# A hybrid decoder layer on one NeuronCore: the first MLP product by Strassen's rule, its outputs spilled to DRAM, the second product in four chunks

## The chip, the core and the metric

The kernel runs on one core of a Trainium2 chip. The metric is the device time of one execution in microseconds (us). Engines are named as in the profile: PE (TensorE; PEld is its weight load), DVE (VectorE), ACT (ScalarE), POOL (GpSimd), SP (SyncE, which here only issues DMAs).

## The reference, cut to what matters

```python
h2 = rmsnorm(x, g_pre_mlp)                     # x: 1024 prompt tokens and 8 decode tokens, 1024 features
f = jnp.square(jax.nn.relu(h2 @ w_ff1)) @ w_ff2    # w_ff1 1024 x 4096, w_ff2 4096 x 1024
x = x + rmsnorm(f, g_post_mlp)

def rmsnorm(x, g):
    return x * lax.rsqrt(jnp.mean(x * x, axis=-1, keepdims=True) + EPS) * g
```

Before this stand the projections, a pooled branch, an mLSTM, a memory attention, the gated merge and the out-projection `merged @ w_out`, whose normalised result is added to x. All is float32.

## The kernel before, in words

All activations lie transposed: features on the 128 partitions (KD = 8 tiles), the N = 1032 tokens along the free axis, cut into NG = 3 groups of G = 344 (`tok[g]`). A float32 product is made of three fp32r passes: each operand is split into a high part (a copy into fp32r) and a low part (the operand minus its high part), and `product` (L573 to L582) issues hi*hi, lo*hi and hi*lo for each 128-deep block into one PSUM bank. So a block of 128 features by 344 tokens over 1024 inputs takes 8 x 3 = 24 matmuls, each with its own weight load.

Weights come as one stream of slabs of 128 x 1024 (512 KB) on SP's queue into two slots of `w_raw`; POOL splits each slab (`split`, L466 to L480: `w_hi` by a multiplication with ones, then `w_lo`), a few by ACT and POOL. SP loads the next slab once the one before it is split.

The MLP runs after the out-projection (units UNIT_OUT on). There ACT takes z out of PSUM and squares it, DVE sums the squares, one matmul with ones per group sums over partitions, ACT takes the root, DVE inverts it and scales (`z_inverse`, `z_scale`), and POOL adds the result to x (L540). Then, for the second norm, ACT squares x tile by tile, PE sums the squares by 24 matmuls with ones (L840), ACT takes the root, DVE inverts it (L1532) and multiplies x by gain and reciprocal (STT, L1181), ACT makes `h_hi`, DVE and POOL make `h_lo` (L1538, L546). The groups follow each other: the first MLP matmul of group 0 waits for group 0's low parts alone.

The first product makes 32 blocks of 128 features, the second 8 blocks; both go in turns, 512 hidden features at a time. `ff1` on PE (L842) issues 4 blocks x 3 groups of 24 matmuls; ACT takes the ReLU (L906), DVE squares (L1547), ACT copies the high part (L1142), DVE makes the low part (L1549), all in SBUF. `ff2` (L848) then multiplies the 512 hidden features: 8 blocks x 3 groups of 12 matmuls, each added by DVE to `acc` (L1559). That is 2304 matmuls for either product, 4608 in all, each 344 columns wide. Every engine works through its own program in order, and semaphores tie them; a group's bank is reused when `s_group_free[g]` says that its reader is done.

At the end `f_last` orders the last groups by token group; ACT squares `acc`, PE sums the squares by 8 matmuls per group (`f_mean`), ACT takes the root, DVE inverts, scales, and DVE and POOL add x1, and SP stores o_y.

## Time and profile before

| | us |
|---|---|
| median of 3 runs | 2166.03 (2163.33 to 2166.05) |
| profiled execution, device time | 2168.67 |
| its span, first to last instruction | 2166.9 |
| PE busy | 2045.7 (94%) |
| DVE, POOL, ACT busy | 957.6, 801.8, 459.7 |
| mean granted TensorE clock | 0.966 |

The span of the profiled execution is 2166.9 us, and 1.8 us lie around it. Busy time counts an engine's instructions; a matmul's record overlaps the next one's, so PE's pace is read from start times or from a stretch's count, not from a single duration. The granted clock is in tenths of full speed: 1.00 is 2.4 GHz and half of it 1.2 GHz.

### The profile page before, as it was taken

The page shows a single profiled execution, that of the slowest core. Times are in us where ns is not written, and L with a number is a line of the kernel's source. Part 1 is how long each engine was busy: PE and PEld are TensorE (multiplying, and loading weights), DVE is VectorE, ACT ScalarE, POOL GpSimd, SP SyncE. Part 2 cuts the span into 40 slices and gives each one's busy share as a digit, 9 for nine tenths or more (in the row PEclk, how much of TensorE's full clock was granted, in tenths as well). Part 3 has the DMA queues.
Part 4 walks back from the last instruction along what each step waited for, and adds up shares of the span by engine and source line. Part 5 has one row for each costly group of instructions (what it writes and reads, how often), then busy time and mean ns, then how long its engine had stood idle before and what let it go on. Part 6 is the DMA issues. An engine that isn't in the chain of part 4 may idle for free.

```text
span 2166.9 us, 32354 instructions
## 1 busy us (share of the span) xinstructions
PE 2045.7 (94%) x12613; PEld 1989.7 (92%) x12613; DVE 957.6 (44%) x1864; ACT 459.7 (21%) x880; POOL 801.8 (37%) x405
## 2 busy tenths in 40 slices
PE   5799999999999999999899989599999999999996
PEld 3799999999999999999789889399999999999995
DVE  6602552045303550255756742964334343343426
ACT  4411220122012211122056422431102011010101
POOL 4553323322333333332512323753434343333433
PEclk8899999999999999999789999799999999999998
DMA  3221331123211331133544331211111111111132
GB/s 137 69 79 44 132 140 50 40 104 134 79 49 60 133 124 40 40 136 127 211 140 140 104 127 39 98 40 49 49 39 50 49 49 40 49 49 49 40 117 79
DMA packets 64140, 180.13 MB, mean 83 GB/s; under 512 B 6648, under 2 KB 22264, under 8 KB 63400
## 3 DMA queue, kind: packets, MB, share of 16 engines
q1 hardware_dynamic: 57664, 154.46, 20.8%
q10 hardware_dynamic: 6376, 24.14, 2.8%
q8 instruction: 86, 1.41, 0.3%
q14 instruction: 14, 0.11, 0.0%
HBM read 141.83 MB, written 36.75 MB: 82 GB/s over the span
## 4 chain that ended last, share of the span: by engine, by line
PE 85%; DVE 9%; issue 2%; ACT 2%; DMA 1%; POOL 1%; SPq 0%; DVEq 0%; ACTq 0%; POOLq 0%
PE bank L580 78%; DVE acc L1181 2%; PE bank L708 1%; PE bank L711 1%; DVE x_in L1181 1%; PE bank L700 1%; PE bank L663 1%; PE bank L706 1%; PE bank L747 1%; DMA x_in<-xT 1%; PE bank L780 0%; PE bank L840 0%; PE bank L687 0%; PE bank L803 0%; PE bank L716 0%
## 5 line engine op out<-in xcount | busy, mean ns | idle before, releaser
L580 PE MATMUL bank<-h_hi,w_hi 128*128 128x344 f32 x2520 | 824.4, 327 | 26.9 <-DVE h_lo L1196 14.2
L580 PE MATMUL bank<-h_lo,w_hi 128*128 128x344 f32 x2520 | 809.5, 321 | 0.0
L580 PE MATMUL bank<-h_hi,w_lo 128*128 128x344 f32 x2520 | 806.8, 320 | 0.0
L477 POOL TENSOR_TENSOR w_hi<-w_raw,ones 128x1024 fp32r<-128x1024 f32 x152 | 288.7, 1900 | 1165.9 <-PE bank L580 1153.2
L580 PEld LDWEIGHTS bank<-h_hi,w_hi 128*128 128x128 f32 x2520 | 477.4, 189 | 33.8 <-issue 16.1
L580 PEld LDWEIGHTS bank<-h_hi,w_lo 128*128 128x128 f32 x2520 | 476.9, 189 | 1.2
L580 PEld LDWEIGHTS bank<-h_lo,w_hi 128*128 128x128 f32 x2520 | 476.9, 189 | 0.0
L479 POOL TENSOR_TENSOR w_lo<-w_raw,w_hi 128x1024 fp32r<-128x1024 f32 x152 | 372.0, 2447 | 11.9
L580 PE MATMUL bank<-f_hi,w_hi 128*128 128x344 f32 x768 | 246.4, 321 | 0.0
L580 PE MATMUL bank<-f_hi,w_lo 128*128 128x344 f32 x768 | 245.4, 320 | 0.0
L580 PE MATMUL bank<-f_lo,w_hi 128*128 128x344 f32 x768 | 245.2, 319 | 0.0
L1559 DVE TENSOR_TENSOR acc<-acc,bank 128x344 f32<-128x344 f32 x192 | 97.1, 511 | 230.0 <-PE bank L580 229.9
L1547 DVE TENSOR_TENSOR sqv<-rl 128x344 f32<-128x344 f32 x96 | 93.0, 969 | 140.1 <-ACT rl L906 139.7
L580 PEld LDWEIGHTS bank<-f_hi,w_hi 128*128 128x128 f32 x768 | 144.4, 188 | 0.8
L580 PEld LDWEIGHTS bank<-f_lo,w_hi 128*128 128x128 f32 x768 | 144.3, 188 | 0.0
L580 PEld LDWEIGHTS bank<-f_hi,w_lo 128*128 128x128 f32 x768 | 144.1, 188 | 0.2
L906 ACT ACTIVATE rl<-bank 128x344 f32<-128x344 f32 x96 | 43.8, 456 | 419.9 <-PE bank L580 419.9
L1549 DVE TENSOR_TENSOR f_lo<-sqv,f_hi 128x344 fp32r<-128x344 f32 x96 | 98.6, 1027 | 53.6 <-ACT f_hi L1142 53.6
L906 ACT ACTIVATE side_t<-bank 128x344 f32<-128x344 f32 x96 | 43.9, 458 | 284.0 <-PE bank L580 284.0
L1319 DVE TENSOR_TENSOR SW<-bank,SW 128x128 f32<-128x128 f32 x32 | 9.3, 292 | 156.7 <-ACT SW L1019 156.7
L1142 ACT ACTIVATE f_hi<-sqv 128x344 fp32r<-128x344 f32 x96 | 47.2, 492 | 117.8 <-DVE sqv L1547 117.8
L906 ACT ACTIVATE o_h<-bank 128x344 f32<-128x344 f32 x40 | 18.3, 458 | 245.0 <-PE bank L580 241.2
(288 smaller groups left out, 2385.0 us busy)
## 6 DMA issues: line engine op xcount, KB each, us to landing
w_raw<-w_stream SPq DMA_DIRECT2D x161, 512.0 KB, 3.3
d_side<-side_t ACTq DMA_DIRECT2D x32, 516.0 KB, 2.6
gates<-d_side SPq DMA_DIRECT2D x24, 344.0 KB, 4.4
dC<-stC SPq DMA_DIRECT2D x32, 256.0 KB, 3.4
qkb<-d_qk SPq DMA_DIRECT2D x32, 256.0 KB, 4.0
o_C_s<-dC SPq DMA_DIRECT2D x32, 256.0 KB, 2.0
x_in<-xT SPq DMA_DIRECT2D x3, 1376.0 KB, 10.9
gates<-d_side SPq DMA_DIRECT2D x8, 516.0 KB, 4.0
```

The costliest lines, as they stand in the source:

```text
L477: pool.tensor_tensor(w_hi[:, slot, :], w_raw[:, slot, :], ones[:, 0:1].to_broadcast([P, 1024]), ALU.mult).then_inc(s_hi_made, 1)
L479: pool.tensor_tensor(w_lo[:, slot, :], w_raw[:, slot, :], w_hi[:, slot, :].bitcast(F32), ALU.subtract)\
L580: last = pe.matmul(out, st, mv, start=i == 0, stop=i == n - 1)
L663: last = pe.transpose(b_tr[r][:, (c % 2) * 256 + k * P:(c % 2) * 256 + (k + 1) * P], src[:, k, c * L:(c + 1) * L], ident[:, :])
L700: last = pe.matmul(b_S[:, 0:L], ks[:, k, :], qs[:, k, :], start=k == 0, stop=k == 1)
L706: pe.matmul(b_N[:, 0:257], SW[:, :], vc, start=True, stop=True)
L906: act.activation(out, bank[g + 3 * second][:, 0:G], func, scale=scale).then_inc(s_group_free[g], 1)
L1142: act.activation(f_hi[:, half, j, tok[g]], sqv[:, g, :], ACT.Copy).then_inc(s_f_hi, 1)
L1181: return dve.scalar_tensor_tensor(out=out, in0=in0, scalar=scalar, in1=in1, op0=op0, op1=op1)
L1547: dve.tensor_tensor(sqv[:, g, :], rl[:, g, :], rl[:, g, :], ALU.mult).then_inc(s_relu_squared, 1)
L1549: dve.tensor_tensor(f_lo[:, half, j, tok[g]], sqv[:, g, :], f_hi[:, half, j, tok[g]].bitcast(F32), ALU.subtract).then_inc(s_f_lo, 1)
L1559: dve.tensor_tensor(acc[:, j, tok[g]], acc[:, j, tok[g]], bank[g + 3 * second][:, 0:G], ALU.add).then_inc(s_group_free[g], 1)
```

## The change

What it does, in the order of time:

- The weights of the MLP lie otherwise in the stream: 32 slabs of w_ff1 (128 output columns each), then 32 of w_ff2 (128 outputs over a quarter of the hidden features).
- After the out-projection POOL makes the sums and low parts of the first four weight combinations before it adds x1. ACT, with each tile's square, also writes x1 times the gain (`s_xg`) into `acc`; the reciprocal of the norm is applied after the ReLU.
- The first product goes by Strassen's rule in 16 pairs of slabs (PAIRS): w_ff1's two halves of inputs and two 128-column tiles against x1's two halves of features and two halves of tokens (HALF = 516, in two pieces of Q4 = 258). Seven products p = 0 to 6 take the place of eight; each is 2 pieces x 4 x 3 = 24 matmuls of 258 columns. The seven activation operands are built once (`build` on DVE, `b_high` on ACT); the weight sums and splits are made per pair (`wc_sum`, `wc_lo` on POOL, `wc_high` on ACT, 512 columns each) in a ring of 8. Product pieces take the 8 PSUM banks in turn.
- ACT copies the pieces of p = 0 to 2 out of PSUM, DVE combines the rest (`combine`: 16 additions from PSUM and 8 STTs max(., 0) * rstd per pair), ACT squares into a staging tile (`make_f`), and SP stores f's two rows to DRAM (`store_f`).
- The second product goes in four chunks of 1024 hidden features (units u = 0 to 31, 8 per chunk). f's rows are loaded back and split again. Units 0 and 1 are done together with the contraction outermost, so that PE can begin with row 0; row 0, 2, 4, 6 of chunk 0 get their low parts from POOL and rows 1, 3, 5, 7 from DVE. The weights are split by ACT (`w2_high`) and POOL (`w2_split`).
- At the end the squares of the result are summed by DVE, and one matmul per group takes the place of eight.
- Several semaphores of other stages are merged into one each, and some small tiles share room with the new ones; the order of their work is kept.

The core of the diff:

```diff
-            for g in range(NG):
-                pe.wait_ge(s_h2_lo, KD // 2 * (g + 1))
-                pe.wait_ge(s_h2_lo_pool, KD // 2 * (g + 1))
...
+            pe.wait_ge(s_x1_std, NG)
+            for i in range(PAIRS):
+                for p in range(7):
+                    n = 7 * i + p
+                    pe.wait_ge(s_wc_lo, n + 1)
+                    for s in range(2):
+                        t = 2 * n + s
+                        if i == 0:
+                            pe.wait_ge(s_b_lo, 2 * p + s + 1)
+                        if t >= 8:
+                            copied, stepped = tile_read(t - 8)
...
+                        product(bank[t % 8][:, 0:Q4],
+                                [(ring_hi[n % RING][:, k * P:(k + 1) * P], ring_lo[n % RING][:, k * P:(k + 1) * P],
+                                  b_hi[p][:, k, sub[s]], b_lo[p][:, k, sub[s]]) for k in range(4)]).then_inc(s_tile, 1)
...
+            for k in range(KD):
+                pe.wait_ge((s_f_row_lo, s_f_row_lo_dve)[k % 2], k // 2 + 1)
+                for u in range(2):
+                    if k == 0:
+                        pe.wait_ge(s_w2_lo, u + 1)
```

POOL, beside PE:

```diff
+            for n in (0, 2, 3):
+                wc_sum(n)
+            for n in range(4):
+                wc_lo(n)
             pool.wait_ge(s_x2_loaded, 16)
...
+            for n in range(4, 7 * PAIRS):
+                wc_sum(n + 1)
+                wc_lo(n)
```

DVE, from the last scaling of z on (the reciprocals of the norm stand in `combine`, before the first "u" step of pair 0):

```diff
+            def build(p):
+                a, op, b = B_OF[p]
+                for s in range(2):
+                    if op is not None:
+                        if p == 6:
+                            dve.wait_ge(s_x1_stored, 16)
+                        dve.tensor_tensor(b_sum[p][:, :, sub[s]], b_quarter(a, s), b_quarter(b, s), op).then_inc(s_b_sum, 1)
+                for s in range(2):
+                    dve.wait_ge(s_b_hi, 2 * p + s + 1)
+                    t = b_quarter(a, s) if op is None else b_sum[p][:, :, sub[s]]
+                    dve.tensor_tensor(b_lo[p][:, :, sub[s]], t, b_hi[p][:, :, sub[s]].bitcast(F32), ALU.subtract).then_inc(s_b_lo, 1)
...
+            dve.wait_ge(s_xg, NG * KD)
+            for p in range(5):
+                build(p)
+            combine(0, 1)
+            build(5)
+            combine(0, 2)
+            build(6)
+            for p in range(3, 7):
+                combine(0, p)
```

ACT in the pairs, in the second product, and SP's wait for pair 1:

```diff
+            for i in range(PAIRS):
+                for p in range(7):
+                    n = 7 * i + p
+                    if i == 0 and p == 0:
+                        b_high(1)
+                        wc_high(4)
+                        wc_high(5)
+                        for q in (2, 3, 4):
+                            b_high(q)
+                    elif i == 0 and p == 1:
+                        b_high(5)
+                    wc_high(n + 6)
+                    if i == 0 and p == 0:
+                        act.wait_ge(s_b_lo, 10)
+                    if p == 0 and i:
+                        make_f(i - 1, 6)
+                    if p < 3:
+                        copy_c(i, p)
...
+            for u in range(24):
+                w2_high(u + 3)
+                f_row_high(8 + u)
+                if u < 8:
+                    for g in range(NG):
+                        take(g, UNIT_FF + u, acc[:, u, tok[g]], second=u == 1)
...
+                elif i == 1:
+                    sp.wait_ge(s_b_lo, 10)
...
+                else:
+                    sp.wait_ge(s_group_ready[2], UNIT_FF + u - 3)
+                sp.dma_start(w2_raw[u % 4], w_stream[SLAB_FF + 32 + u]).then_inc(s_w2_loaded[u % 4], 16)
```

## Rows read from the trace of the kernel before

**Rows 1.** the page: busy shares, and granted clock in 40 slices
```profile
PE 2045.7 (94%) x12613; PEld 1989.7 (92%) x12613; DVE 957.6 (44%) x1864; ACT 459.7 (21%) x880; POOL 801.8 (37%) x405
...
PEclk8899999999999999999789999799999999999998
```

**Rows 2.** windows view, two MLP stretches: stretch, busy us (xinstructions) per engine, PEclk
```profile
1430.00:1620.00 190.00, 190.00 (x1210) 189.83 (x1209) 82.17 (x104) 28.88 (x61) 79.06 (x34) 1.00 0.15 48
...
1820.00:2120.00 300.00, 300.00 (x1908) 299.69 (x1907) 115.51 (x160) 36.31 (x77) 113.61 (x52) 1.00 0.17 58
```

**Rows 3.** timeline, PE, around the MLP: start, us, what, count [idle <-releaser]
```profile
1395.36 7.89 PE L840 MATMUL bank<-sq,ones 128*128 128x344 f32 x16 [18.01 <-ACT sq L1128]
1402.83 0.58 PE L580 MATMUL bank<-h_hi,w_hi 128*128 128x344 f32 x1
...
2141.18 1.32 PE L889 MATMUL bank<-sqv,ones 128*128 128x344 f32 x4
```

**Rows 4.** timeline, PE, products of the memory keys, 256 columns wide
```profile
87.48 0.28 PE L580 MATMUL bank<-m_hi,w_hi 128*128 128x256 f32 x1
...
90.09 0.28 PE L580 MATMUL bank<-m_lo,w_hi 128*128 128x256 f32 x1
```

**Rows 5.** timeline, DVE, from out-projection to MLP
```profile
1374.63 9.43 DVE L1181 SCALAR_TENSOR_TENSOR acc<-acc,vec,rstd 128x344 f32<-128x344 f32 x8
1383.98 2.29 DVE L1532 RECIPROCAL rstd<-rstd0b 128x344 f32<-128x344 f32 x1
1386.31 8.10 DVE L1181 SCALAR_TENSOR_TENSOR acc<-x_in,vec,rstd 128x344 f32<-128x344 f32 x8
1394.33 1.79 DVE L1538 TENSOR_TENSOR h_lo<-acc,h_hi 128x344 fp32r<-128x344 f32 x4
```

**Rows 6.** timeline, POOL, same stretch
```profile
1353.98 4.57 POOL L540 TENSOR_TENSOR x_in<-x_in,acc 128x344 f32<-128x344 f32 x4 [16.18 <-DVE acc L1181]
...
1376.80 8.89 POOL L540 TENSOR_TENSOR x_in<-x_in,acc 128x344 f32<-128x344 f32 x8 [0.45 <-DVE acc L1181]
```

**Rows 7.** groups by line and shape, DVE: xcount, then busy us, mean ns
```profile
L1559 DVE TENSOR_TENSOR acc<-acc,bank 128x344 f32<-128x344 f32 x192 | 97.1, 511 | 230.0 <-PE bank L580 229.9
...
L1345 DVE TENSOR_TENSOR num<-num,bank 128x257 f32<-128x257 f32 x32 | 13.3, 416 | 0.0
...
L1408 DVE TENSOR_TENSOR win_b<-win_a 128x1032 f32<-128x1032 f32 x1 | 2.8, 2819 | 0.0
...
L1224 DVE TENSOR_TENSOR A_row<-bb,mm_ 4x1032 f32<-4x1032 f32 x1 | 1.2, 1214 | 0.0
```

**Rows 8.** source view of L1181: ns min/median/max, first and last start
```profile
L1181 DVE SCALAR_TENSOR_TENSOR acc<-acc,vec,rstd x48: 564/1218/2094, 1353.3 to 2161.4; 128x344 f32<-128x344 f32 x48
```

**Rows 9.** groups by line and shape, POOL
```profile
L479 POOL TENSOR_TENSOR w_lo<-w_raw,w_hi 128x1024 fp32r<-128x1024 f32 x152 | 372.0, 2447 | 11.9
...
L493 POOL TENSOR_TENSOR m_lo<-mem_in,m_hi 128x2048 fp32r<-128x2048 f32 x1 | 4.7, 4694 | 12.0 <-ACT m_hi L942 12.0
```

**Rows 10.** source view of L540, POOL: ns min/median/max
```profile
L540 POOL TENSOR_TENSOR x_in<-x_in,acc x24: 905/1180/1199, 1354.0 to 1384.8; 128x344 f32<-128x344 f32 x24
```

**Rows 11.** groups by line and shape, ACT
```profile
L952 ACT ACTIVATE w_hi<-w_raw 128x1024 fp32r<-128x1024 f32 x7 | 7.4, 1052 | 8.6 <-PE bank L580 8.6
...
L956 ACT ACTIVATE mem_in<-bank 128x256 f32<-128x256 f32 x8 | 3.0, 381 | 16.2 <-PE bank L580 16.2
```

**Rows 12.** DMA view: queue share; issues with KB each, us to landing
```profile
q1 hardware_dynamic: 57664, 154.46, 20.8%
...
w_raw<-w_stream SPq DMA_DIRECT2D x161, 512.0 KB, 3.3
...
x_in<-xT SPq DMA_DIRECT2D x1, 4128.0 KB, 12.4
```

**Rows 13.** chain that ended last, end of kernel: start, us, what
```profile
2154.71 7.26 DVE acc L1181 x8
...
2162.82 0.43 DVE x_back L1587
```

More of the change, by code:

```diff
@@ L440, in _ @@
             sp.dma_start(x_in[:, :, :], xT).then_inc(s_x2_loaded, 16)
[L441 to L446 removed]
+            for n in range(SLAB_MERGE + 12, SLAB_FF):
+                slab(n, n % 2, n - 1)
@@ new lines, in _ @@
+            pair(0)
+            pair(1)
+            for i in range(PAIRS - 1):
+                if i + 2 < PAIRS:
+                    pair(i + 2)
+                if i == PAIRS - 2:
+                    w2_slab(0)
+                store_f(i)
+            for r in range(4):
+                sp.wait_ge(s_tile, 14 * (PAIRS - 1) + 2 * r + 2)
+                if r == 2:
+                    w2_slab(1)
+                if r >= 2:
+                    sp.wait_ge(s_f_row_hi, 2 * r - 2)
+                sp.dma_start(f0_raw[:, 2 * r:2 * r + 2, :], d_f[2 * r:2 * r + 2].rearrange("a p t -> p a t"))\
+                    .then_inc(s_f_row[r % 2], 16)
@@ L864, in _, with f_mean @@
+            for u in range(2, 28):
+                if u % 8 == 0:
+                    pe.wait_ge(s_f_row_lo, 4 + u)
+                pe.wait_ge(s_w2_lo, u + 1)
+                for g in range(NG):
+                    ff2_group(u, g)
+            def f_mean(g):
+                pe.wait_ge(s_f_summed, 16 + 4 * g)
+                pe.matmul((b_I, b_U, b_S)[g][:, 0:G], ones[:, :], frb[:, tok[g]], start=True, stop=True).then_inc(s_f_ssq, 1)
             for g in range(NG):
-                pe.wait_ge(s_h2_lo, KD // 2 * (g + 1))
@@ L866, in _ @@
[L866 to L867 removed]
+                for u in range(28, 32):
                     if g == 0:
[L869 to L879 removed]
@@ L1133, in _ @@
             x1_root(2)
-            h2_hi(2)
-            act.wait_ge(s_x1_stored, 16)
-            def ff1(t, half, count, order):
-                for i, (j, g) in enumerate(order):
-                    take(g, t + j, rl[:, g, :], ACT.Relu, second=order is first_blocks and j == 1)
-                    act.wait_ge(s_relu_squared, count + i + 1)
-                    act.activation(f_hi[:, half, j, tok[g]], sqv[:, g, :], ACT.Copy).then_inc(s_f_hi, 1)
-            ff1(UNIT_FF, 0, 0, first_blocks)
@@ new lines, in f_root @@
+            def f_root(g):
+                root(frb[:, tok[g]], (b_I, b_U, b_S)[g][:, 0:G], s_f_ssq, g + 1, s_f_std)
+            for u in range(24):
+                w2_high(u + 3)
+                f_row_high(8 + u)
+                if u < 8:
+                    for g in range(NG):
+                        take(g, UNIT_FF + u, acc[:, u, tok[g]], second=u == 1)
+            for i in range(24):
+                if i % 3 == 0 and i < 15:
+                    w2_high(27 + i // 3)
+                square_f(i)
+                if i in (18, 22):
+                    f_root((i - 18) // 4)
@@ new lines, in _, with ff2_add @@
+            for p in range(3, 7):
+                combine(PAIRS - 1, p, "u")
+            def ff2_add(u, g, second=False):
+                dve.wait_ge(s_group_ready[g], UNIT_FF + u + 1)
+                dve.tensor_tensor(acc[:, u % 8, tok[g]], acc[:, u % 8, tok[g]], bank[g + 3 * second][:, 0:G], ALU.add)\
+                   .then_inc(s_group_free[g], 1)
+            for u in range(8, 24):
+                for g in range(NG):
+                    if u < 16:
+                        dve.wait_ge(s_group_free[g], UNIT_FF + 8)
+                    ff2_add(u, g)
@@ new lines, in add_square @@
+            def add_square(i):
+                j, g = f_last[i]
+                dve.wait_ge(s_f_squared, i + 1)
+                if j == 0:
+                    dve.tensor_copy(frb[:, tok[g]], fsq[:, i % 3, :]).then_inc(s_f_summed, 1)
+                else:
+                    prev = max(q for q in range(i) if f_last[q][1] == g)
+                    dve.wait_ge(s_f_summed, prev + 1)
+                    dve.tensor_tensor(frb[:, tok[g]], frb[:, tok[g]], fsq[:, i % 3, :], ALU.add).then_inc(s_f_summed, 1)
```

697 lines of the change are left out of this document (418 added, 279 removed), and 3 rows, old and new, of the table C_STEPS.

## The prediction

> **What bounds the kernel now.** I read the page first: PE is busy 94% of the span, the others 44% or less [rows 1]. The windows view of the MLP then shows 190.0 of 190 us busy and 300.0 of 300, at granted clock 1.00 [rows 2]: the MLP is PE's issue rate and nothing else. Its count gives the pace: 1210 matmuls in 190 us, 1908 in 300, so 157.0 ns for 344 columns. By the timeline the MLP's first matmul starts at 1402.8 and the last group ends at 2141.2 [rows 3]: 738 us, of which 4608 x 0.157 = 723.5 are products. Two places are bound by something else: 1384 to 1403, where DVE inverts, scales and splits group 0 while PE has at most ones-matmuls [rows 3, 5], and the tail from 2141.2 to 2166.9 on DVE [rows 13]. So the reader asks three things: what a narrower matmul costs, who else gets near the pace of PE, and what the two edges become.
>
> **Width of a matmul.** 2304 matmuls of 344 columns become 16 x 7 x 24 = 2688 of 258. That the columns fall by an eighth is arithmetic; the time needs a row. Products 256 wide, also fp32r and back to back, start 23 times in 90.09 - 87.48 = 2.61 us: 113.5 ns [rows 4]. The slope between that and 157.0 at 344 is 0.494 ns per column, so 258 costs 114.4 ns. Ends: 114.4, and 121.0 if the excess over 2.4 GHz is that of 344 (157.0 - 143.3 = 13.7 ns) and not that of 256 (6.8). I take 114.4, the nearest row by far. One of the 112 products (24 matmuls) then takes 2.75 us and a pair 19.2. Dense, 2688 x 0.1144 = 307.5 us against 361.7: a gross gain of 54.2.
>
> The Trainium skill (TensorE: Matmul & The Clock Gate, "Wait — 56ns, not 53.3ns?") puts back-to-back matmuls at the columns over 2.4 GHz plus about 2.5 ns. By that 258 columns cost 110.0 ns, 11.8 us less than my sum over 2688. The trace doesn't agree for fp32r: it has 157.0 where that gives 145.8.
>
> **Do the others keep up inside a pair (19.2 us)?** POOL has 12 two-input operations of 512 columns. 1024 take 2.45, 2048 take 4.69, 344 alone 0.905 [rows 9, 10], so 512 about 1.24: 14.9 us, with waits 15.7. ACT has 7 splits of 512 (1.05 for 1024, so 0.55), 6 copies and 8 squares of 258 (0.38 for 256) [rows 11]: 9.2. DVE has 16 additions from PSUM (0.416 for 257) [rows 7], 0.36 in sequence: 5.8; and 8 STTs with both inputs in SBUF. Alone one of 344 takes 0.56, median 1.22, at most 2.09 [rows 8]; with POOL beside it the two engines alternate, 8 STTs in 9.43 us against 8 POOL additions in 8.89 [rows 5, 6]. So a STT here is bounded below by 0.47 and costs one POOL operation when POOL is dense, 1.24 + 0.27 (what POOL's median 1.180 adds to its 0.905 [rows 10]). 8 x 1.5 = 12.0 at the upper end, 1.1 each as my value: DVE 5.8 + 8.8 + 1.2 of waits = 15.8, at most 19.0. POOL rises to 15.7 + 8 x 0.27 = 17.9. Both stay under 19.2, with little to spare. Rings (8 weight slots, 8 banks) let them lag 11 us and more, so I cost all of this at nothing. The cover is PE's 19.2 us; each us a pair lasts longer costs about 15 us. Two 512 KB slabs and two stored rows per pair are 2 MB in 19.2 us; the queue moves 154.46 MB in 20.8% of the span, 343 GB/s when busy [rows 12]: 6 us, hidden.
>
> **The front edge.** POOL starts adding x1 at 1353.98 now [rows 6]. In the change it has three sums and four low parts first, the last after ACT's root of group 1 and two more splits: about 1357, and they collide with DVE's two-input sums. The chain behind it stays DVE's scaling of group 2 (1374.63 to 1384.0 [rows 5]), since POOL catches up on group 1, where a split stood. Last addition 1386, ACT's square and scaled copy 1 us, 1 us for collisions: all of `s_xg` at T0 = 1388 (1386 to 1391). Gone are the reciprocals and scalings that DVE did from 1384 on.
>
> Then DVE builds. An operation is 128 x 1032 with two SBUF inputs: 1.21 us alone, 2.82 behind POOL [rows 7]. Ledger from T0, in DVE's order: builds 0 to 4, 18 operations at 1.2 plus 2.4 for first splits and collisions, 24.0 (POOL has four operations then, for `wc_sum(7)` waits for pair 1). Pair 1 is loaded only after build 4: 1 MB, 5 us (512 KB land in 3.3 [rows 12]), 29.0. Behind it queue POOL's sum, 1.3; ACT's `wc_high(7)` and, queued behind that on ACT, the copy of p = 1, 1.0; DVE's two additions, 0.9: 32.2. Build 5, two operations at 1.55, 35.3; additions 36.2; build 6, four, 42.4; two additions 43.3; three reciprocals at 2.3 [rows 5], 50.2; STTs and additions of p = 3 to 6 up to the last one that frees a bank for product 10, 8.6: about 59. PE does ten products (27.5 us) in this time and waits for 31.5. The ends: 50 with no collisions and a quick load, 67 with POOL in the way of half the builds (12 x 0.8 more). From product 10 PE runs dense: 102 x 2.746 = 280.0. The first product ends at 1388 + 59 + 280 = 1727.
>
> **The hand-over.** Chunk 0's rows come back while pair 15 runs. `store_f(14)` stands ahead of them on SP; ACT takes rows 4 and 5 before `w2_high(1)`, and POOL row 2 before `w2_split(1)`, which PE needs for unit 1 at its first step. From the start of pair 15: rows 0, 1 at 10 us, rows 2, 3 at 13, slab 1 at 14.5, rows 4, 5 at 18, ACT 20.7, POOL 23.1, against PE's 20.7: 3 us (0 to 13, at half the load rate). After units 0 and 1 PE asks for ACT's takes of unit 1; on ACT they are queued behind `w2_high(4)`, whose slab SP may load only when unit 0 is done, and row 9 behind it on the queue: 3.4 + 1.1 + 1.1 + 0.5 = 6.1 against 1.4 of work, a stall of 4.7, with a dip of the clock 5.5 (3 to 9). Then 2304 x 0.157 = 361.7, and 0.9 for two means: the last group ends at 1727 + 3 + 5.5 + 361.7 + 0.9 = 2098.1.
>
> **The tail.** From the last group but one (3.8 us before the end) DVE has an addition, a sum, a reciprocal, 4 STTs, addition, sum, 4 STTs, sum, 3 additions, reciprocal, 8 STTs, 3 additions. At 0.42, 2.3, 0.9 and 0.45 (7.26 us for 8 STTs [rows 13]) it ends 20.7 us behind the last group, and 3.6 for the store as now: 24.3 (now 25.7). Span 2122.4, execution 2124.2 with the 1.8 around it. The profiled execution is 2.6 above the median of the runs, so 2121.5.
>
> **Rivals.** (1) *DVE or POOL sets the pair.* If each STT waits out a POOL operation and loses its turn again, it costs the largest row, 2.09 [rows 8]: 5.8 + 16.7 + 1.2 = 23.7 us per pair, 4.5 over PE's, over 14.6 pairs 66 us: 2187, slower than before. It decides from 19.2 + 44.5 / 14.6 = 22.2 us per pair. For it: DVE and POOL both have to run at over 80% on a port that rows 5 and 6 show them alternating on. Against: STT and POOL addition together took 1.15 us, not 2.09, which stood behind a 1024-wide operation. The Trainium skill (SBUF — State Buffer, "Who interferes with whom") says that a DVE instruction with two SBUF inputs contends with GpSimd's reads and that one of them waits; the trace agrees (2.82 against 1.21). (2) *The mild form.* POOL's 512-wide operation costs 1.4, since its fixed part is larger, or a matmul 121.0 ns: the pair takes 20.3 to 20.7, and 15 x 1.1 to 1.5 and a longer opening make 2144. (3) *The opening hides better.* DVE's builds run at 1.21 and the hand-over stalls are nil: 59 becomes 50 and 8.5 go: 2104. (4) *It doesn't do what it says*: a narrower matmul would not be faster in proportion, since each has its weight load. PEld is busy 1989.7 us beside PE [rows 1]. Rows 4 exclude it at 256 columns.
>
> **How the numbers follow.** Forecast 0.60: 2121.5, own range 2106 to 2140. Mild form 0.17. Better opening 0.10. Slower pair 0.13, of which most ends above the time before: slower 0.11. The 8-in-10 range takes in the better opening and the mild form with the longer hand-over, 2103 to 2156. A change under 0.2% (4.3 us) counts as the same, about what the measurement can tell: 0.03. Faster 0.86.
>
> **What would show it.** In the profile after: 258-wide matmuls starting 114.4 ns apart; `wc_lo` on POOL 1.24 us; pairs of 19.2 us with no idle PE from product 10 on, else rival 1 or 2, and the idle time's releaser tells which engine; first product's matmul at 1390 to 1392, product 10 at 1447, second product from 1727 to 1730; one idle stretch of some 5 us after unit 1; 24 us of tail. The prediction is wrong if PE waits in every pair, or if the opening is over 70 us.

## The result and the profile after

The changed kernel takes 2145.92 us (median of 4 runs, 2144.65 to 2147.58) against 2166.04 (2163.33 to 2167.76): ratio 0.9907 [0.9891, 0.9924]. It is faster, by 20.1 us where 44.5 were forecast. Its profiled execution took 2146.56, its span is 2144.4, the mean granted clock 0.964. Two of the changed kernel's variants below had one run each at a far lower granted clock (0.57 and 0.83), and their medians leave that run out.

The page of the changed kernel, busy time and two of the lines by slices, as [rows 1] of before:

```profile
PE 2007.3 (94%) x12955; PEld 1950.6 (91%) x12955; DVE 952.8 (44%) x1952; ACT 599.5 (28%) x1124; POOL 907.9 (42%) x518
...
PE   5799999999999999999899989769999989999995
...
PEclk8899999999999999999879999889999999999997
```

The page alone says little: PE is at 94% as before. The windows view by stage says where to look (the opening, the dense first product, the start of the second, its long middle; against [rows 2]):

```profile
core 0: us, PE busy (x) PEld busy (x) DVE busy (x) ACT busy (x) POOL busy (x), PEclk, DMA share, GB/s
1386.00:1445.00 59.00, 39.57 (x240) 38.23 (x240) 50.85 (x49) 23.64 (x37) 26.41 (x16) 0.80 0.25 99
1447.00:1717.00 270.00, 270.00 (x2255) 270.00 (x2255) 188.99 (x330) 121.46 (x287) 217.75 (x166) 1.00 0.31 109
1738.00:1796.00 58.00, 50.82 (x296) 50.28 (x295) 13.42 (x14) 20.26 (x33) 30.45 (x12) 0.91 0.29 102
1796.00:2067.00 271.00, 271.00 (x1727) 271.00 (x1726) 34.00 (x69) 57.20 (x68) 105.19 (x44) 1.00 0.29 102
```

The second line decides the case. PE has no idle time in 270 us and the clock is full, so nobody holds PE up; yet 270.00 / 2255 = 119.7 ns per 258-column matmul, not 114.4. The last line has the old pace, 271.00 / 1727 = 156.9 ns for 344 columns.

The groups of DVE and POOL in that stretch (count | busy us, mean ns | idle before), against [rows 7 to 10]:

```profile
L1421 DVE SCALAR_TENSOR_TENSOR c_t<-c_t,rstd 128x258 f32<-128x258 f32 x108 | 111.6, 1072 | 0.0
L1810 DVE TENSOR_TENSOR c_t<-c_t,bank 128x258 f32<-128x258 f32 x84 | 34.9, 424 | 76.0 <-PE bank L741 42.6 <-ACT c_t L1322 31.5 <-issue 1.9
...
L688 POOL TENSOR_TENSOR w_lo<-w_lo_raw,w_hi 128x512 fp32r<-128x512 f32 x34 | 45.3, 1340 | 13.1 <-ACT w_hi L1277 13.1
```

A STT of 258 columns takes 1.07 us (1.1 was my value), an addition from PSUM 0.42, a POOL operation of 512 columns 1.34 in this group and 1.32 to 1.43 in the others (1.24 was my value).

DVE through the opening (start, length; in brackets the idle time before and who ended it), against [rows 5]:

```profile
1385.24 2.43 DVE L1776 TENSOR_TENSOR bA_raw<-acc 128x1032 f32<-128x1032 f32 x2 [2.67 <-ACT acc L1296]
...
1407.26 2.38 DVE L1780 TENSOR_TENSOR bC_lo<-bC_raw,bC_hi 128x1032 fp32r<-128x1032 f32 x2
1416.95 0.76 DVE L1810 TENSOR_TENSOR c_t<-c_t,bank 128x258 f32<-128x258 f32 x2 [7.31 <-ACT c_t L1322]
1417.63 4.05 DVE L1780 TENSOR_TENSOR bD_lo<-acc,bD_hi 128x1032 fp32r<-128x1032 f32 x2
...
1429.09 6.62 DVE L1794 RECIPROCAL rstd<-rstd0b 128x344 f32<-128x344 f32 x3
```

T0, the time at which all of x1 times the gain is there, is 1385.24 (forecast 1388); the builds, the 7.31 us behind the load of pair 1 with ACT's copy at its end, and the three reciprocals stand as in the ledger. Product 10 starts at 1445.07: an opening of 59.8 us. One thing the ledger does not have: in the opening the mean granted clock is 0.80 (first line of the windows view), and the 240 matmuls of the ten products take 39.6 us and not the 28.7 of full speed. PE's waits in the opening are therefore 20.3 us and not the 31.5 of the forecast; the total came out because DVE's chain, and not PE, sets it.

PE's timeline at the four places where it waits in the second product, and the last line of all, against [rows 3]:

```profile
1738.48 0.32 PE L1038 MATMUL bank<-f_hi,w_x_hi 128*128 128x344 f32 x1
...
1742.12 0.65 PE L1038 MATMUL bank<-f_hi,wcD_hi 128*128 128x344 f32 x1 [2.06 <-POOL wcD_lo L710]
...
1770.29 0.63 PE L741 MATMUL bank<-f_hi,w_hi 128*128 128x344 f32 x1 [5.12 <-ACT acc L1068]
1770.71 0.49 PE L741 MATMUL bank<-f_hi,w_lo 128*128 128x344 f32 x1
1771.00 0.49 PE L741 MATMUL bank<-f_lo,w_hi 128*128 128x344 f32 x1
...
2075.63 0.40 PE L741 MATMUL bank<-f_hi,w_hi 128*128 128x344 f32 x1 [0.70 <-DVE acc L1846]
...
2109.51 0.85 PE L1051 MATMUL bank<-frb,ones 128*128 128x344 f32 x2 [2.60 <-DVE frb L1862]
...
2119.13 0.31 PE L741 MATMUL bank<-f_lo,w_hi 128*128 128x344 f32 x1
```

Behind the longer waits the matmuls start 0.29 us apart for a while (1770.71 to 1771.00) and not 0.157; the windows view has the granted clock between its two levels there:

```profile
1742.00:1746.00 4.00, 3.88 (x15) 3.88 (x16) 4.00 (x2) 0.00 (x0) 4.00 (x3) 0.57 0.22 90
1766.00:1776.00 10.00, 5.71 (x20) 5.74 (x21) 0.00 (x0) 5.28 (x7) 7.51 (x4) 0.67 0.48 182
```

So the wait of 5.12 us costs 8.1: 5.3 from where the next matmul would have started (1764.85 + 0.16 to 1770.29), and 2.8 by which the 144 matmuls behind it take longer (25.4 us for 22.6). Read the same way, the wait of 2.06 us costs 3.9 and that of 2.60 about 5. The last group ends at 2119.4, and 25.0 us later the span ends.

The balance from 1384.0 in both traces, where DVE's last scaling of z ends before the change (with the change it starts at the same 1374.6 and ends at 1382.6): the products of the first half fall from 361.7 us (2304 x 0.157) to 322.1 (112 products), 39.6 less. What is not a product at full speed up to the dense part grows from 18.8 us (1384.0 to 1402.8 [rows 3, 5]) to 32.3 (1.2 to T0, and 59.8 less ten products of 2.87; 10.8 of it is the lower clock of the opening), 13.5 more. What is not a product in the rest grows from 14.9 (738.4 - 723.5) to 19.3 (381.0 - 361.7), 4.4 more. Net 21.7 by the last group's end.

### The profile page after: what moved, and what is told of

Its sections match the earlier page's. It is cut to its first block, busy times and chain, and to the rows that moved or that the text cites. A ratio compares the mean times of both kernels' runs of the same rounds, so it can differ in the third digit from the quotient of the medians.

```text
span 2144.4 us, 33425 instructions
## 1 busy us (share of the span) xinstructions
PE 2007.3 (94%) x12955; PEld 1950.6 (91%) x12955; DVE 952.8 (44%) x1952; ACT 599.5 (28%) x1124; POOL 907.9 (42%) x518
## 4 chain that ended last, share of the span: by engine, by line
PE 82%; DVE 10%; issue 3%; ACT 2%; DMA 2%; POOL 1%; SPq 0%; DVEq 0%; ACTq 0%; POOLq 0%
PE bank L741 73%; DVE acc L1421 2%; PE bank L869 1%; PE bank L872 1%; DVE x_in L1421 1%; PE bank L1038 1%; DMA f_raw<-d_f 1%; PE bank L861 1%; PE bank L824 1%; PE bank L867 1%; PE bank L908 1%; DMA x_in<-xT 1%; DVE bA_lo L1780 0%; POOL x_in L697 0%; PE bank L941 0%
## 5 line engine op out<-in xcount | busy, mean ns | idle before, releaser
L741 PE MATMUL bank<-h_hi,w_hi 128*128 128x344 f32 x1752 | 577.7, 330 | 24.6 <-DVE h_lo L1436 14.7
L741 PE MATMUL bank<-h_lo,w_hi 128*128 128x344 f32 x1752 | 563.5, 322 | 0.0
L741 PE MATMUL bank<-h_hi,w_lo 128*128 128x344 f32 x1752 | 561.4, 320 | 0.0
L741 PEld LDWEIGHTS bank<-h_hi,w_hi 128*128 128x128 f32 x1752 | 332.4, 190 | 30.6 <-DVE h_lo L1436 15.3
L741 PEld LDWEIGHTS bank<-h_hi,w_lo 128*128 128x128 f32 x1752 | 332.3, 190 | 1.1
L741 PEld LDWEIGHTS bank<-h_lo,w_hi 128*128 128x128 f32 x1752 | 332.1, 190 | 0.0
L615 POOL TENSOR_TENSOR w_lo<-w_raw,w_hi 128x1024 fp32r<-128x1024 f32 x90 | 217.4, 2415 | 7.1
L741 PE MATMUL bank<-f_hi,w_hi 128*128 128x344 f32 x384 | 125.2, 326 | 5.8 <-ACT acc L1068 5.1
L1421 DVE SCALAR_TENSOR_TENSOR c_t<-c_t,rstd 128x258 f32<-128x258 f32 x128 | 126.2, 1027 | 0.0
L741 PE MATMUL bank<-f_hi,w_lo 128*128 128x344 f32 x384 | 124.3, 324 | 0.0
```

The lines of the kernel that those rows point to most:

```text
L615: pool.tensor_tensor(w_lo[:, slot, :], w_raw[:, slot, :], w_hi[:, slot, :].bitcast(F32), ALU.subtract)\
L741: last = pe.matmul(out, st, mv, start=i == 0, stop=i == n - 1)
L1421: return dve.scalar_tensor_tensor(out=out, in0=in0, scalar=scalar, in1=in1, op0=op0, op1=op1)
```

## The experiments

All of them run beside the kernel before on their chip (medians there 2165.6 to 2167.0). Their profiles have the same work ahead of T0, and T0 still lies anywhere between 1380.3 and 1389.7. So a single profile's span scatters by some us for reasons that no edit touches, and I also compare the span behind T0: 759.2 us for the changed kernel (2144.4 - 1385.2).

| kernel | median us | ratio to before | span behind T0 |
|---|---|---|---|
| changed kernel | 2145.92 | 0.9907 [0.9891, 0.9924] | 759.2 |
| takes (ACT's copies out of PSUM) of units 0 and 1 together | 2137.78 | 0.9877 [0.9840, 0.9914] | 751.3 |
| mean one unit later | 2148.47 | 0.9914 [0.9887, 0.9940] | 760.3 |
| copies ahead of splits | 2143.04 | 0.9880 [0.9828, 0.9931] | 755.1 |
| plain order of units 0 and 1 | 2144.37 | 0.9899 [0.9863, 0.9935] | 760.0 |
| rows split by POOL alone | 2146.07 | 0.9909 [0.9882, 0.9936] | 757.0 |
| scaling spread at the end | 2141.35 | 0.9888 [0.9862, 0.9913] | 751.0 |
| five edits | 2120.57 | 0.9787 [0.9765, 0.9810] | 733.6 |
| two more POOL operations per pair | 2149.82 | 0.9927 [0.9907, 0.9947] | 765.3 |
| four more | 2177.27 | 1.0050 [1.0031, 1.0068] | 789.8 |

### What a matmul costs by its width

Series of 96 matmuls, each series one line of this form, its width and data changed:

```diff
+for i in range(96): last = pe.matmul(bank[2][:, 0:258], wt[i % 8], X[:, 516 * (i % 8 % 7):516 * (i % 8 % 7) + 258], start=i == 0, stop=i == 95)
```

> Measures the disputed cost by itself: runs of 96 fp32r matmuls back to back on otherwise idle engines, one run for each width and start in SBUF; all the rest of the computation is left out. In the changed kernel 258 columns start 119.8 ns apart where the forecast had 114.4. Theory A (the start of the moving operand: pieces of 258 floats begin at multiples of 1032 bytes): 258 columns on 2048-byte starts take 114.4, and 256 columns on the 2064-byte stride take about 119. Theory B (a step just above 256 columns, whatever the start): 256 stays at 113.5 on any start, 258 takes 120 on any start, and 260 and 264 the same as 258. Theory C (other engines' traffic in the changed kernel costs it): 258 takes 114.4 here on every start, on the line between 256 and 344.

The source view of its lines at 240, 254, 256, 258, 344 and 512 columns (durations of one, first and last start, form):

```profile
L148 PE MATMUL bank<-X,W x96: 272/274/278, 286.7 to 297.3; 128*128 128x240 f32 x96
...
L146 PE MATMUL bank<-X,W x96: 277/282/283, 275.4 to 286.5; 128*128 128x254 f32 x96
...
L110 PE MATMUL bank<-X,W x96: 283/283/283, 35.9 to 47.3; 128*128 128x256 f32 x96
L112 PE MATMUL bank<-X,W x96: 278/282/287, 47.4 to 58.8; 128*128 128x258 f32 x96
...
L138 PE MATMUL bank<-X,W x96: 317/322/334, 206.0 to 221.3; 128*128 128x344 f32 x96
...
L144 PE MATMUL bank<-X,W x96: 387/389/397, 253.6 to 275.1; 128*128 128x512 f32 x96
```

The starts are rounded to 0.1 us here, which is 1 ns in the quotient, so I take them from the timeline view, which has hundredths: start to start it is 112.0 ns at 240 columns, 117.7 at 254, 120.0 at 256 and at 258, 160.3 at 344, 227.1 at 512. At 128 and 192 it is 111.4, and a series of 344 columns with its data laid out otherwise gave 157.8. None of the theories fits as a whole: of B, 258 at 120 on any start is right, and 256 at 113.5 on any start is wrong. C is excluded, since on idle engines 258 columns cost the same 120.0 ns as in the kernel. Up to 240 columns the price is almost flat, 111.4 to 112.0 ns. Above it rises to a line of 0.418 ns per column (227.1 - 120.0 = 107.1 for 256 columns; 2.4 GHz gives 0.417), some 13 ns above the columns at 2.4 GHz. The 258-column matmul lies on the line. Floor and line meet between 240 and 254 columns, just below my nearest row.

### Is it the layout? Two more such kernels

The series repeat the three-pass order, the strides and the addresses of both products; the second one shifts the moving data:

```diff
+for i in range(96): last = pe.matmul(bank[1][:, 0:256], z([0, 2048, 0][i % 3] + 128 * (i // 3 % 8), 128), z([4112, 4112, 6160][i % 3] + 256 * (i // 3 % 8), 256), start=i == 0, stop=i == 95)
```

> The matmul price by itself, with the rest of the computation left out (the outputs are not the reference's). Series of 96 dense fp32r matmuls in the kernel's three-pass order (high weights on high data, low weights on high data, high weights on low data, eight or four blocks in turn), at 256, 258, 260 and 344 columns, with the data laid out as in the memory products (256 columns per block, contiguous), as in the first MLP product (blocks of 516, halves of 258) and shifted by 2 to 128 columns, with the two passes on one weight side by side, and with one weight alone. Theory A (the layout of the moving data sets the price): the memory products' own layout gives 113.5 ns again, the kernel's 258-column layouts give 119.8, and a shift or another stride moves 256 by some ns. Theory B (the order of the weights sets it): the three-pass order gives 113.5 at 256 in every layout, and one weight alone or another order differs. Theory C (the 113.5 ns of the memory products was not the dense price of 256 columns): every 256-column series gives 116 to 120 as in the run before, and 258 gives 119.8 to 121 whatever the layout.

> The matmul price by itself again, with the rest of the computation left out (the outputs are not the reference's): in the run before, one of ten 256-column layouts cost 112.6 ns per matmul and the rest 116.8 to 120.0; that one started its moving data 16 elements behind the round address. Here the moving data are shifted by 0 to 80 elements at 256 columns and at 258 columns (the kernel's layout), the two parts (high, low) are shifted one without the other, the weights are shifted, and the cheap case is repeated in another place. Theory A (the address decides): the cheap case is repeated at 112.6, a shift of 16 gives about 114 at 258 too, and which part has to be shifted is seen; a kernel laid out so would win back up to 2688 x 6 ns = 16 us. Rival B (it is not the address but how a series happens to fall in with the weight loads): the cheap price turns up in other places or not at all, 258 columns cost 119.8 to 121 at every shift, and no layout wins anything.

The series of the line just shown in the first kernel, then the same addresses twice in the second (source views; the two fences are two kernels):

```profile
L122 PE MATMUL bank<-Z x96: 276/276/279, 116.1 to 126.8; 128*128 128x256 f32 x96
```

```profile
L118 PE MATMUL bank<-Z x96: 279/279/284, 92.5 to 103.6; 128*128 128x256 f32 x96
...
L132 PE MATMUL bank<-Z x96: 276/282/288, 171.7 to 183.1; 128*128 128x258 f32 x96
...
L162 PE MATMUL bank<-Z x96: 276/276/276, 343.2 to 354.0; 128*128 128x256 f32 x96
```

Read in hundredths, one and the same series costs 113.4, 117.8 and 113.3 ns (the 112.6 of the expectation is the rounding; its cheap price is the 113.5 of the memory products [rows 4]). By the source only the place in the program and the output bank (1, 5 and 3) differ. The 31 series of 256 columns in the two kernels, nearly all with data or weights laid out otherwise, lie between 113.3 and 120.0, with no rule in the address that I could find. At 258 columns all eleven shifts gave 118.8 to 121.0. So rival B of the last run holds in what it says of the prices: 256 columns cost anything from the cheap price to the dear one, 258 only the dear one, and no layout that I tried wins the 16 us. What decides at 256 stays open; how a series falls in with the weight loads is argued and not shown.

### Are DVE, ACT and POOL cover? More work for POOL

```diff
+                if i and p in (1, 4):
+                    for _ in range(1):
+                        extra.append(n)
+                        pool.tensor_tensor(ring_lo[n % RING], t, ring_hi[n % RING].bitcast(F32), ALU.subtract).then_inc(s_pool_extra, 1)
+                        pool.wait_ge(s_pool_extra, len(extra))
                 pool.tensor_tensor(ring_lo[n % RING], t, ring_hi[n % RING].bitcast(F32), ALU.subtract).then_inc(s_wc_lo, 1)
```

With `range(2)` it is four more per pair.

> Every pair from the second on has two more POOL operations of 512 columns (the low parts of products 2 and 5 are made twice, which changes no value). POOL is busy 218.3 of 270.5 us in the steady stretch, 16.2 us of a pair of 20.1; two more at 1.3 make 18.9. Theory A (PE sets the pair, the rest is cover): hidden, 2144 to 2150, no idle PE in the pairs. Rival B (the pair is already near POOL's pace because of its waits on ACT): 1 us per pair, 2160.

> The same with four more POOL operations per pair, 16.2 + 5.3 = 21.5 us of work and some waits, against PE's 20.1. Theory A: POOL sets the pair; 1.4 to 2.2 us more in each of 15 pairs, less what the ring of eight weight blocks lets it lag at the start: 2165 to 2178, with PE idle in front of POOL's low parts in each pair. Rival B (POOL's operations get dearer as DVE and POOL both fill the pair): 1.5 us and more per operation, 22.2 and up: over 2180. Rival C: the lag of the ring hides it, under 2155.

The steady stretch with two more by windows (columns as above) and, by the lines view, its STTs; then the same stretch with four more, with the waits of PE and ACT from 1450 to 1730 (us in total, times, longest):

```profile
1447.00:1717.00 270.00, 270.00 (x2256) 270.00 (x2255) 211.88 (x329) 119.02 (x282) 258.93 (x192) 1.00 0.30 105
```

```profile
L1429 DVE SCALAR_TENSOR_TENSOR c_t<-c_t,rstd 128x258 f32<-128x258 f32 x110 | 138.5, 1298 | 0.0
```

```profile
1447.00:1717.00 270.00, 256.29 (x2115) 254.21 (x2116) 193.22 (x304) 104.58 (x265) 264.19 (x200) 1.00 0.29 103
...
PE bank L749 <- ACT c_t L1330: 14.9, 13, 1.4
...
ACT w_hi L1285 <- POOL w_lo_raw L683: 80.9, 31, 5.1
ACT wcA_hi L1285 <- POOL wcA_raw L683: 49.8, 17, 5.3
```

With two more, POOL is busy 96% and DVE's busy time rises from 189.0 to 211.9 for as many operations (329 and 330), and PE has still no idle time: the pairs hide it. The rise is in the STTs alone, whose inputs are both in SBUF, 1298 ns instead of 1072; the additions from PSUM stay at 410 to 424 ns. The median is 3.9 us higher and the span behind T0 6.1, and that stands outside the dense pairs: 2.1 in the opening (61.9 us), 4.0 in the second product, where PE's wait for POOL's second weight block is 5.92 us instead of 2.06. With four more POOL is the bound at 98%, a pair takes 21.6 us (PE's waits stand 21.54 to 21.60 apart) instead of 20.1, and the kernel is slower than before. Theory A in both, in the second near the upper end of its range. The reader should see whom PE's line names: ACT, an engine that is busy 39% of the time. The next two lines say why: ACT's copy stands in its queue behind splits that wait for POOL's sums. The releaser of a wait is not yet the bound; one follows it back to the engine that has no idle time.

### The parts of the change: order of units 0 and 1, rows by two engines

Undone, each alone:

```diff
-            for k in range(KD):
-                pe.wait_ge((s_f_row_lo, s_f_row_lo_dve)[k % 2], k // 2 + 1)
-                for u in range(2):
...
+            pe.wait_ge(s_f_row_lo, 4)
+            pe.wait_ge(s_f_row_lo_dve, 4)
+            for u in range(2):
+                pe.wait_ge(s_w2_lo, u + 1)
+                for g in range(NG):
...
+                    product(bank[g + 3 * u][:, 0:G],
```

> The changed kernel with one part undone: units 0 and 1 of the second product run group by group again, not contraction-outermost, and so start when all eight rows of chunk 0 are split. In the changed kernel's trace the last low part of those rows is made at 1748.8 and the product begins at 1738.5, so PE would wait 10.3 us more there, with about 2 us of lower clock behind it. Theory A (mine): it is given back, since unit 0's groups are finished one by one, their takes are done before unit 1 ends, and both the idle time of 2.06 us at the second weight block and the 8.1 us after unit 1 go: the time stays within 3 us of the changed kernel, 2143 to 2149. Rival B: the stall after unit 1 remains, since it hangs on ACT's queue and not on the order of the products: 10 us slower, 2154 to 2158.

PE's waits from 1700 to 2080 in the timeline of that kernel, all of them:

```profile
1746.70 0.66 PE L741 MATMUL bank<-f_hi,w_x_hi 128*128 128x344 f32 x1 [11.22 <-POOL f_lo L705]
...
2073.46 0.40 PE L741 MATMUL bank<-f_hi,w_hi 128*128 128x344 f32 x1 [0.70 <-DVE acc L1842]
```

One wait of 11.22 us stands in the place of two of 2.06 and 5.12 with their low clock; from the first product's end to the last group it is 381.9 us against 381.0. Theory A (its median is 2144.4): the early start of unit 0 was given back in full after unit 1, because the takes don't keep step with it.

```diff
-                pe.wait_ge((s_f_row_lo, s_f_row_lo_dve)[k % 2], k // 2 + 1)
+                pe.wait_ge(s_f_row_lo, k + 1)
...
+            for r in range(4):
+                f_row_lo(r, r + 1)
             w2_split(1)
+            for r in range(4, 8):
+                f_row_lo(r, r + 1)
```

> The changed kernel with one part undone: all eight rows of chunk 0 get their low part on POOL, none on DVE. POOL then has four rows (4 x 2.4 us) instead of two before the second weight block, so that block is ready at 1731.0 + 9.6 + 2.4 = 1743.0 instead of 1742.1, and rows 4 to 7 follow every 2.4 us, up to 1752.6, ahead of PE, which asks for one every 2.83 us from 1750 on. Theory A (mine): 1 us more at the second weight block, and no other stall: 2146 to 2148, the same within the error. Rival B: the rows come later than PE asks, a wait at each of rows 4 to 7: 5 us slower, 2151.

2146.07; the wait for the second weight block is 3.06 us instead of 2.06, and no new one stands at rows 4 to 7. As expected: with rows asked for every 2.83 us, one engine at 2.4 to 2.6 keeps up. But the second product takes 378.8 us, 2.1 less than in the changed kernel and not 1 more. The windows view behind its wait in the hand-over shows a difference in the clock (the changed kernel's line from 1742.00 to 1746.00 has 0.57):

```profile
1744.00:1748.00 4.00, 3.65 (x23) 3.65 (x24) 4.00 (x3) 0.84 (x2) 4.00 (x3) 1.00 0.08 32
```

Here the clock stayed full behind the longer wait, and behind the wait after unit 1 (4.99 us) the next 144 matmuls lost 1.5 us and not 2.8. So what the lower clock adds to one and the same wait varies by 1 to 2 us from one profile to the next, and the size of a single stall isn't known better than that.

### The waits one by one

ACT takes units 0 and 1 before the next slab's split:

```diff
-                if u < 8:
+                for v in ((0, 1) if u == 0 else (u,) if 1 < u < 8 else ()):
                     for g in range(NG):
-                        take(g, UNIT_FF + u, acc[:, u, tok[g]], second=u == 1)
+                        take(g, UNIT_FF + v, acc[:, v, tok[g]], second=v == 1)
```

> One change to the changed kernel: ACT takes unit 1 of the second product out of PSUM right behind unit 0, ahead of the split of slab 4 and row 9. If the idle PE after unit 1 (5.1 us in the trace) comes from the takes being queued behind that split: the idle time falls to under 1 us, PE keeps its clock, and the kernel is 8 us faster (5.3 of wait, 2.8 of matmuls at the low clock): 2138. Rival: PE waits there for slab 2 or row data as well, then 1 to 3 us of idle time remain and the gain is under 5 us.

2137.78. As expected: the wait after unit 1 is gone, and from the first product's end to the last group's end it is 372.8 us, 8.1 less: the whole stall with its low clock, and nothing takes its place.

PE's mean of group 1 one unit later:

```diff
-                    if g and u == 29:
+                    if g and u == 28 + g:
```

> One change to the changed kernel: PE issues the mean of group 1 one group later (behind unit 30 of group 2). The trace has PE idle for 2.6 us before it, and the 48 matmuls behind it take 9.5 us where 7.5 is the pace. If this wait is what costs: no idle PE there, the last group ends 4.8 us earlier, and the kernel is 4 to 5 us faster: 2141. Rival: DVE's scaling sets the end and not PE, then PE ends earlier but the kernel's time stays within 1 us of 2146.

The time stays (2148.47), and neither half is as I wrote it: PE still waits, and its last group ends no earlier (the second product takes 382.7 us against 381.0, nearly all of the difference ahead of unit 4). PE's timeline of that kernel in the last 60 us:

```profile
2112.52 0.66 PE L741 MATMUL bank<-f_hi,w_hi 128*128 128x344 f32 x1 [3.03 <-DVE acc L1846]
...
2130.08 1.52 PE L1051 MATMUL bank<-frb,ones 128*128 128x344 f32 x2 [7.77 <-DVE frb L1862]
```

The wait of 2.60 us for DVE's row sum became one of 3.03 us for DVE's addition, on which the next group's bank hangs. The bound there is DVE: behind group 0's reciprocal (2.30) it has 4 STTs, an addition and a sum, 4 STTs, 3 additions, an addition and the sum that PE waits for, in one piece of 12.3 us (2097.1 to 2109.5 in the changed kernel's trace), and PE's requests come 3.8 us apart. So the cure is in DVE's order:

```diff
-                if i in (18, 22):
-                    q = (i - 18) // 4
-                    y_inverse(q)
-                    y_scale(q, range(4))
...
+                if i == 18:
+                    y_inverse(0)
+                    y_scale(0, range(1))
+                elif i in (19, 20):
+                    y_scale(0, range(3 * i - 56, 3 * i - 53))
+                elif i == 21:
+                    y_scale(0, range(7, KD))
+                    y_inverse(1)
```

> One of the five edits alone: DVE's scaling of groups 0 and 1 in the last units is spread (one, three, three and one of group 0's eight behind the additions that follow each other), so that the row sums of group 1 are ready when PE asks for their mean, and group 1's inverse comes before the last group. Theory A: the wait of 2.60 us before the mean of group 1 goes with the 2.5 us of repeated start and low clock behind it, and the tail behind the last group falls from 25.0 to 23 us: 7 us in all, 2139. Rival B: as in the run with the moved mean, another wait of about 3 us for DVE takes its place, and the time stays at 2146.

2141.35. The second product takes 375.0 us, 6.0 less, with a wait of 0.58 us in that place, and the tail is 22.9, 2.1 less. But 2.4 of the 6.0 stand ahead of unit 4, which the edit doesn't touch (a hand-over of 1.69 us of wait and another course of the clock). The edit's own share is 3.6 us there, where theory A had 5.1, and the tail as it said: 5.7 us together, of which the medians show 4.6. Rival B is excluded.

ACT's two copies of the opening ahead of its two weight splits (their old places, further down, are emptied; not shown):

```diff
                     elif i == 0 and p == 1:
                         b_high(5)
+                        copy_c(0, 1)
+                        copy_c(0, 2)
+                        b_high(6)
```

> One change to the changed kernel: in pair 0 ACT copies the pieces of p = 1 and 2 and splits operand 6 before it waits for the sum of weights 7. Theory of the ledger (DVE's chain sets the opening, and its 7.3 us of idle time before the first addition comes from ACT queued behind pair 1's load): product 10 starts 6 to 7 us earlier (1438 instead of 1445) and the kernel takes 2139. Rival (the load of pair 1 sets the opening by itself, through POOL's sums, which PE needs for product 7): product 10 moves by 0 to 2 us and the time by as little.

The profile has T0 at 1389.7, 4.4 us later than the changed kernel's, and product 10 at 1444.6: the opening took 54.9 us instead of 59.8. DVE's wait before the first addition is 2.98 us instead of 7.31. So 4.9 us where the theory of the ledger had 6 to 7 and the rival 2 at most; the time of 2139 wasn't reached (2143.0). The runs scatter too much (2135.5 to 2146.9) to show 4 us by themselves.

Both of these, the takes, weight block 1 ahead of rows 4 and 5 on ACT, and the reciprocals of groups 0 and 1 in DVE's waiting time:

```diff
+                        if p == 6:
+                            w2_high(1)
                         f_row_high(2 * p - 8)
                         f_row_high(2 * p - 7)
-            w2_high(1)
...
+            dve.wait_ge(s_x1_std, 1)
+            dve.reciprocal(rstd0[:, tok[0]], rstd0b[:, tok[0]])
             dve.wait_ge(s_xg, NG * KD)
             for p in range(5):
                 build(p)
+            dve.wait_ge(s_x1_std, 2)
+            dve.reciprocal(rstd0[:, tok[1]], rstd0b[:, tok[1]])
```

> Five edits of the order of instructions, each against one wait in the trace of the changed kernel. (1) ACT takes units 0 and 1 together before it waits for the next slab: 8.1 us, as measured alone. (2) ACT's two copies for the opening go ahead of two weight splits: product 10 starts 4.9 us earlier after the last scaled column, as measured alone. (3) DVE inverts groups 0 and 1 before and behind its first builds, in time in which it waits: 2.3 to 4.6 us more in the opening. (4) ACT splits weight block 1 ahead of rows 4 and 5: the idle 2.06 us with 1.8 us of lower clock go, 3.9. (5) DVE's scaling of group 0 and 1 in the last units is spread so that the row sums of group 1 are ready when PE asks, and the inverse of group 1 comes before the last group: 5.1 us of PE and about 2 us of the tail. Theory A (each wait is its own): the sum, 26 to 28 us: 2119. Rival B (one wait hides the next, as the moved mean showed): half of it, 2132. Rival C: the front edge is not DVE's queue but the load of pair 1, so that (3) gives nothing: 2122.

2120.57 us: 45 us under the kernel before, 25 under the changed one. PE's waits over 0.25 us after 1700 in its timeline, all of them:

```profile
2057.23 0.40 PE L741 MATMUL bank<-f_hi,w_hi 128*128 128x344 f32 x1 [0.70 <-DVE acc L1850]
...
2089.67 0.43 PE L741 MATMUL bank<-f_hi,w_hi 128*128 128x344 f32 x1 [0.58 <-DVE acc L1850]
...
2100.30 0.85 PE L1051 MATMUL bank<-frb,ones 128*128 128x344 f32 x2 [2.82 <-DVE frb L1866]
```

The opening is 51.5 us (1386.8 to 1438.3), 8.3 less: 4.9 by the copies as measured alone, so 3.4 by the reciprocals, which rival C had at nothing. The second product takes 365.4, 15.5 less, of it 12.0 ahead of unit 4, as the takes and weight block 1 were to give, and 3.5 near the end for the forecast 5.1; the tail is 22.9, 2.1 less. That is theory A: 25.4 us by the medians, for its 26 to 28. The first product is 293.8 (293.4 in the changed kernel): this order of work doesn't touch its 119.8 ns.

## Why the prediction was half right

The direction held, and so did the wide range (2103 to 2156); the forecast's own range (2106 to 2140) did not, and of the gain of 44.5 us less than half came, 20.1. The step that failed is the first one, the price of a matmul of 258 columns: 114.4 ns in the forecast, 119.8 in the kernel and 120.0 alone, 13.4 of the 24.4 us. Next comes a term put at nothing, PE's waits near the end, 6.0 us. Forecast against the trace, term by term (negative: the trace is quicker); the differences add up to 24.3 of the 24.4 us:

| term | forecast | trace | us |
|---|---|---|---|
| T0 | 1388 | 1385.2 | -2.8 |
| opening to product 10 | 59 | 59.8 | +0.8 |
| 102 products | 280.0 | 293.4 | +13.4 |
| hand-over | 3 | 3.9 | +0.9 |
| after unit 1 | 5.5 | 8.1 | +2.6 |
| 2304 matmuls of 344, means | 362.6 | 363.0 | +0.4 |
| waits near the end | 0 | 5.1 and 0.9 | +6.0 |
| tail | 24.3 | 25.0 | +0.7 |
| profile to median | -0.8 | +1.5 | +2.3 |

*Width of a matmul.* The step that failed most, by its size. I drew a line between 113.5 ns at 256 columns [rows 4] and 157.0 at 344 [rows 2] and took the near end because 258 is next to 256. The micro kernels show that 256 columns can cost anything from 113.3 to 120.0 ns, that my row had the cheapest of these, close to the flat price of narrower matmuls (112.0 at 240), and that 258 always lies on the line above. The other end of my bounds, 344's excess over 2.4 GHz carried down to 258, was the right reading: 107.5 + 13.7 = 121.2 (the prediction has 121.0, and 114.4 where its own line gives 114.5) against 119.8 measured. A slope of 0.494 ns per column where 2.4 GHz gives 0.417 could have told me that the two rows don't belong to one law. The Trainium skill (TensorE: Matmul & The Clock Gate, "Wait — 56ns, not 53.3ns?") would have 110.0 ns here, an estimate by its formula; the trace has 119.8, 9.8 more, and for these fp32r matmuls the excess over the columns is 12.3 ns at 258 columns and not 2.5.

*Do the others keep up?* Right. POOL's operation cost 1.32 to 1.43 and not 1.24 (its own rows, 0.905 at 344, 2.45 at 1024 and 4.69 at 2048 columns, lie on lines that give 1.29 to 1.32 at 512; half of 2.45 was taken), DVE's STT 1.07, and both stayed under PE's pair, which was itself 20.1 us long. Two more operations still fit, four don't; so rival 1, the slower pair, was some 3 POOL operations away. Its mechanism exists: with POOL at 96% DVE's same instructions took 12% longer, all of it in the STTs. By the Trainium skill (SBUF — State Buffer, "Who interferes with whom") a DVE instruction with two SBUF inputs contends with a POOL instruction that reads SBUF, and the run agrees, with 211.9 against 189.0 us.

*The front edge* and *the opening*. Both right within 3 us, and the ledger's order of events too; PE's lower clock in the opening (10.8 us) wasn't in it, and PE waits for DVE only 0.26 us before product 10, so that it is hidden by DVE's chain, but only just. What the ledger had as given, the copies behind the weight splits and the reciprocals after the builds, was 8 us to be had.

*The hand-over* and *after unit 1*. Mechanism right in both: POOL's second weight block, then ACT's takes behind a slab. The second was 2.6 us short, 0.6 of it in the wait and 2.0 in the matmuls at the lower clock behind it, for which I had allowed 0.8 us. By the run with the rows on POOL alone, 1 to 2 us of that vary from one profile to the next.

*The waits near the end.* The step that was missing. In the timeline of the kernel before, PE waits for none of the first two means, and 0.55 us for the last; I carried 0.9 for the means over from there. But the change moves the row sums from PE's ones-matmuls to DVE, into the same queue as the scaling; that is a wait added on PE, with 12 us of DVE's work queued ahead of it, and I didn't follow it. The run with the scaling spread takes 3.6 of the 5.1 us away and so shows the cause.

*The rivals.* The mild form (2144, at 121.0 ns or 1.4 us) is the nearest to what happened, 2145.9, by its matmul and not by POOL, which stayed hidden. That the two times agree so closely is in part luck: its opening didn't grow, and the 6.0 us of waits near the end aren't in it. It had 0.17 because I gave the matmul's price to the nearest row.

## What to carry to other kernels

A price beside an edge is read from the far side too: where two rows give a slope that the clock doesn't give, they may not lie on one line, and a series of 96 matmuls of the width in question settles it before the kernel is rewritten (120.0 ns alone, 119.8 in the kernel). When a change moves work from one engine to another, follow the new owner's queue at each place where somebody waits for it, up to the last microseconds. An early start (contraction outermost) is worth nothing until what consumes it is early too: here 8 us lay in the order of six takes.

## What the runs showed of the hardware

In these series an fp32r matmul with its load of a 128 x 128 weight block costs at least 111.4 ns start to start, almost the same at 128, 192 and 240 columns (111.4 to 112.0). From 258 to 512 columns it costs 10 to 15 ns more than its columns at 2.4 GHz (118.8 to 121.0 at 258, 157.0 to 157.8 at 344, 226.7 to 227.1 at 512; one series of 344 columns gave 160.3, 17 more). So a product cut narrower gains less than its columns: seven products of 258-column pieces cost 39.6 us less than eight in 344-column pieces, where an eighth of 361.7 is 45.2. At exactly 256 columns the series gave 113.3 to 120.0, one and the same series 113.3, 113.4 and 117.8 in different places, and why is open. Behind waits of PE of 2 to 5 us the granted clock fell to the lower level for a while in most profiles, but not in all: 0.57 behind 2.06 us in the changed kernel, 1.00 behind 3.06 us in the kernel with the rows on POOL alone.
